# Banded attention by 64-query chunks of eight heads, keys stored in band order, output projections one group late

## The reference

```python
q, gate = jnp.split(rms_norm(x, norm_g) @ w_in, 2, axis=-1)   # 32 query heads of 64
q = partial_rope(q.reshape(B, L, B_Q_HEADS, B_HEAD_DIM), cos, sin)
o = swa_sink_attention(q, k_sh, v_sh, sinks)                  # 4 key heads, 8 query heads each
return x + (o * jax.nn.silu(gate)) @ w_out
# in swa_sink_attention: NC = 8 chunks of 64 queries; a query sees the 16 meta keys,
# its own chunk of keys and the two chunks before it; the softmax has one more term, exp(sink)
e = jnp.exp(sc - m)
return e / (jnp.sum(e, axis=-1, keepdims=True) + jnp.exp(sink - m))
```

## Time and profile before

| | us |
|---|---|
| median of 3 runs | 3215.2 (3215.03 to 3229.05) |
| profiled execution, its own time | 3217.8 |
| span of its records | 3215.9 |
| PE busy (17876 matmul records) | 3057.8 (95%) |
| PEld busy | 2605.3 (81%) |
| DVE busy | 1511.1 (47%) |
| ACT busy | 1021.2 (32%) |
| POOL busy | 1213.6 (38%) |
| mean granted TensorE clock | 0.978 |

### The profile page before, as it was taken

How to read it: one execution, slowest core, us unless ns; L and a number is a source line. 1 busy time by engine, 2 the same in 40 slices (tenths; PEclk the granted TensorE clock), 3 DMA queues, 4 the chain that set the end, 5 groups by cost and what they waited for, 6 DMA issues and landing times.

```text
span 3215.9 us, 44287 instructions
## 1 busy us (share of the span) xinstructions
PE 3057.8 (95%) x17876; PEld 2605.3 (81%) x17876; DVE 1511.1 (47%) x2731; ACT 1021.2 (32%) x1572; POOL 1213.6 (38%) x888
## 2 busy tenths in 40 slices
PE   7999999999999888999999999799999999999986
PEld 7999999999999887877778777777777777787754
DVE  6444343434435376445454556723233234354556
ACT  4322223132222353323233233532323232233342
POOL 4344343434434242231423324644343343344421
PEclk9999999999999999999999999799999999999998
DMA  4121221212222121121211213222222222221211
GB/s 159 67 92 66 79 79 66 93 66 79 79 79 79 66 73 53 53 79 40 92 53 55 77 40 125 92 92 79 79 81 85 84 79 75 83 82 66 80 64 66
DMA packets 36958, 247.63 MB, mean 77 GB/s; under 512 B 3970, under 2 KB 4115, under 8 KB 8212
## 3 DMA queue, kind: packets, MB, share of 16 engines
q1 hardware_dynamic: 35728, 241.37, 22.1%
q10 hardware_dynamic: 1028, 3.44, 0.3%
HBM read 240.60 MB, written 4.19 MB: 76 GB/s over the span
## 4 chain that ended last, share of the span: by engine, by line
PE 79%; DVE 13%; DVEq 3%; issue 2%; ACT 2%; DMA 0%; ACTq 0%; SPq 0%; POOL 0%
PE pj L281 17%; PE pj L285 17%; PE pj L287 17%; PE pj L312 5%; PE pj L316 5%; PE pj L314 5%; DVE xl L359 2%; DVE arena L405 2%; PE pa L503 1%; PE pa L465 1%; DVEq L407 1%; PE pj L842 1%; PE pa L851 1%; PE pa L865 1%; DVE arena L617 1%
## 5 line engine op out<-in xcount | busy, mean ns | idle before, releaser
L1952 POOL TENSOR_TENSOR wl<-raw,wh 128x512 fp32r<-128x512 f32 x884 | 1213.4, 1403 | 1967.0 <-ACT wh L257 1967.0
L281 PE MATMUL pj<-xh,wh 128*128 128x264 f32 (+2 forms) x3792 | 1121.9, 343 | 20.6 <-POOL wl L1952 16.2
L285 PE MATMUL pj<-xl,wh 128*128 128x264 f32 (+2 forms) x3792 | 1083.9, 333 | 13.9 <-DVE xl L359 13.9
L287 PE MATMUL pj<-xh,wl 128*128 128x264 f32 (+2 forms) x3792 | 1078.9, 331 | 0.0
L257 ACT ACTIVATE wh<-raw 128x2048 fp32r<-128x2048 f32 x221 | 423.2, 1915 | 1026.6 <-PE pj L287 602.4
L281 PEld LDWEIGHTS pj<-xh,wh 128*128 128x128 f32 x3792 | 654.2, 192 | 100.0 <-issue 32.7
L285 PEld LDWEIGHTS pj<-xl,wh 128*128 128x128 f32 x3792 | 653.0, 192 | 86.5 <-DVE xl L359 21.2
L287 PEld LDWEIGHTS pj<-xh,wl 128*128 128x128 f32 x3792 | 653.5, 192 | 65.7
L338 DVE TENSOR_TENSOR acc<-pj,acc 128x512 f32<-128x512 f32 (+1 forms) x336 | 233.3, 696 | 209.9 <-PE pj L316 208.5
L312 PE MATMUL pj<-oh,wh 128*128 128x264 f32 (+1 forms) x1024 | 311.4, 345 | 19.6 <-DVE ol L732 11.1
L316 PE MATMUL pj<-oh,wl 128*128 128x264 f32 (+1 forms) x1024 | 307.4, 341 | 0.0
(11 more groups left out here) (271 smaller groups left out, 2776.1 us busy)
## 6 DMA issues: line engine op xcount, KB each, us to landing
raw<-in_stream SPq DMA_DIRECT2D x221, 1024.0 KB, 4.8
acc<-in_x SPq DMA_DIRECT2D x8, 528.0 KB, 9.3
out_y<-acc SPq DMA_DIRECT2D x8, 512.0 KB, 2.9
arena<-in_mem ACTq DMA_DIRECT2D x2, 1024.0 KB, 7.0
cst<-in_cst SPq DMA_DIRECT2D x1, 448.0 KB, 13.7
cos<-in_cos_a SPq DMA_DIRECT2D x1, 264.0 KB, 13.8
sin<-in_sin_a SPq DMA_DIRECT2D x1, 264.0 KB, 14.0
cos<-in_cos_b ACTq DMA_DIRECT2D x1, 264.0 KB, 2.9
```

What stands on the lines that cost most here:

```text
L281: pe.matmul(pj[:, pu, b, 0:m], whk, xh[:, k, a:a + m], start=(k == 0), stop=False)
L285: pe.matmul(pj[:, pu, b, 0:m], whk, xl[:, k, a:a + m], start=False, stop=False)
L287: ins = pe.matmul(pj[:, pu, b, 0:m], wlk, xh[:, k, a:a + m], start=False, stop=(k == KD - 1))
L1952: pool.tensor_tensor(wl[:, j, at], raw[:, j, at], wh[:, j, at].bitcast(F32), ALU.subtract).then_inc(s_part if c < LO_PARTS - 1 else s_lo, 1)
```

## The change

Attention now goes by 64-query chunks, with all 8 query heads of a key head in one slot: 8 chunks per g, 32 in all. The keys are stored in extended form (`B_K`), four blocks of 16 meta keys followed by 128 keys, so that the band of a chunk (16 + 3 x 64 = 208 keys, fewer for the first two chunks) is one contiguous range; the values are stored in two forms, blocks of 128 keys (`B_v1`) and blocks of 64 + 16 (`B_v2`). The sink is an extra column of the scores in PSUM, so that maximum, exponential and sum take it along. The weights are divided before they are transposed, and the output is computed with features on partitions. A slot does the output of chunk i-2, the transposes of i-1 and the scores of i; slots stand at every 6th k (g = 0, 3) or every 8th (g = 1, 2), the first at k = 7 of the first gate tile. All four query tiles of a group come first, then the gate tiles with the slots, then the output projection of the group before it; each output sum runs over four 128-feature parts where it ran over two, so there are 64 sums where there were 128. Of the diff, the allocation of tiles, the reordering of weights on the host, the waits of ACT's tile order and the old functions (printed above) are left out.

```diff
+B_CH = SEQ // CHUNK
+B_BAND = NMETA + 3 * CHUNK
+B_PW = B_BAND + 2
...
-B_OUTS = 8 + 32
+B_TILES, B_OUTS = 48, 96
...
+        def b_band(c):
+            if c < 2:
+                return 0, P - CHUNK * c, B_BAND - P + CHUNK * c
+            return (P + NMETA) * (c // 2) + (NMETA - P - NMETA if c % 2 == 0 else -CHUNK), 0, B_BAND
+
+        def b_block1(c):
+            if c == 0:
+                return None
+            return (0, c // 2 - 1) if c % 2 == 0 else (CHUNK + NMETA, c // 2)
+
+        def b_block2(c):
+            if c < 2:
+                return (P, CHUNK + NMETA, 0) if c == 0 else (CHUNK, NMETA, 0)
+            return (P if c % 2 == 0 else 0), CHUNK + NMETA, c - 1
...
+        def b_extend(dve, out, x):
+            dve.tensor_copy(as3(out, NQ)[:, :, NMETA:], as3(x[:, 0:SEQ], NQ))
+            for j in range(NQ):
+                dve.tensor_copy(as3(out, NQ)[:, j, 0:NMETA], x[:, SEQ:T])
 
         def kv_dve(dve):
...
-                    for b in range(2):
-                        dve.tensor_copy(B_k[64 * b:64 * b + 64, 2 * c + a, :], B_x[64 * a:64 * a + 64, :])
+                    b_extend(dve, B_K[64 - 64 * a:128 - 64 * a, c, 1, :], B_x[64 * a:64 * a + 64, :])
...
+            for c in range(2):
+                evac_scaled(dve, B_x, U_KV + 2 + c, c, T).then_inc(s_evac, 1)
+                dve.drain()
+                b_extend(dve, B_ve[c], B_x)
...
+        B_POS = [[7 + 6 * i for i in range(10)], [7 + 8 * i for i in range(10)], [7 + 8 * i for i in range(10)],
+                 [7 + 6 * i for i in range(10)]]
+
+        def b_slot(g, i):
             def f(pe):
+                c, n = i - 2, B_CH * g + i - 2
+                if 0 <= c < B_CH:
+                    pe.wait_ge(s_btf, n + 1)
+                    if n >= 2:
+                        pe.wait_ge(s_bo, n - 1)
+                    full, (_, rows, slot) = b_block1(c), b_block2(c)
                     for a in range(2):
+                        out = (bank1, bank3)[c % 2][64 * a:64 * a + 64, 0:2 * P]
+                        if full is not None:
+                            pe.matmul(out, B_v1[:, full[1], B_HD * g:B_HD * (g + 1)], B_pt1[:, 2 * P * a:2 * P * (a + 1)],
+                                      start=True, stop=False)
+                        ins = pe.matmul(out, B_v2[0:rows, slot, B_HD * g:B_HD * (g + 1)],
+                                        B_pt2[0:rows, 2 * P * a:2 * P * (a + 1)], start=full is None, stop=True)
                     ins.then_inc(s_bpv, 1)
+                c, n = i - 1, B_CH * g + i - 1
+                if 0 <= c < B_CH:
+                    pe.wait_ge(s_bnorm, n + 1)
...
+                    for v in range(4):
+                        if full is not None:
+                            pe.transpose(bank[2][:, P * v:P * (v + 1)], B_p[:, v, full[0]:full[0] + P], ident)
+                        ins = pe.transpose(bank[3][0:rows, P * v:P * (v + 1)], B_p[:, v, at:at + rows], ident)
                     ins.then_inc(s_bt, 1)
+                c, n = i, B_CH * g + i
+                if c < B_CH:
...
+                        pe.wait_ge(s_bq, 4 * g + 4)
+                    at, lo, w = b_band(c)
+                    for mp in range(2):
+                        for a in range(2):
+                            h = slice(64 * a, 64 * a + 64)
+                            ins = pe.matmul(B_sc[:, 2 * a + mp, lo:lo + w], B_qc[h, c, P * mp:P * (mp + 1)],
+                                            B_K[h, g // 2, (a + g) % 2, at:at + w], start=True, stop=True)
                     ins.then_inc(s_bs, 1)
...
+        def b_slot_act(act, g, i):
+            c, n = i - 1, B_CH * g + i - 1
+            if 0 <= c < B_CH:
+                act.wait_ge(s_bt, n + 1)
...
+                    act.activation(B_pt1, bank[2], ACT.Copy)
...
+                act.activation(B_pt2[0:rows, :], bank[3][0:rows, :], ACT.Copy)
...
+                for v in range(4):
+                    act.activation(B_p[:, v, lo:B_BAND + 1], B_sc[:, v, lo:B_BAND + 1], ACT.Exp, scale=B_scale,
+                                   bias=B_nb[:, v:v + 1], accum_out=B_sm[:, v:v + 1])
...
+        def b_slot_dve(dve, g, i, meanwhile=None):
+            c, n = i - 2, B_CH * g + i - 2
+            if 0 <= c < B_CH:
+                dve.wait_ge(s_bpv, n + 1)
+                dve.tensor_copy(B_qc[:, c, :], (bank1, bank3)[c % 2][:, 0:2 * P]).then_inc(s_bo, 1)
+            c, n = i, B_CH * g + i
+            if c < B_CH:
+                lo = b_band(c)[1]
+                dve.wait_ge(s_bs, n + 1)
+                dve.reduce_max(B_mx, B_sc[:, :, lo:B_BAND + 1], AX_X)
                 dve.drain()
+                dve.tensor_scalar(B_nb, B_mx, -B_scale, None, ALU.mult).then_inc(s_bnb, 1)
+            if meanwhile is not None:
+                meanwhile()
+            if c < B_CH:
+                dve.wait_ge(s_bexp, n + 1)
+                dve.reciprocal(B_rc, B_sm)
                 dve.drain()
+                for v in range(4):
+                    dve.tensor_scalar(B_p[:, v, lo:B_BAND], B_p[:, v, lo:B_BAND], B_rc[:, v:v + 1], None, ALU.mult)
                 dve.drain()
+                dve.sem_inc(s_bnorm, 1)
+
+        def b_out(pe, t, u, o_wait, at, hooks={}):
+            for j in range(4):
+                pe.wait_ge(s_hi, t + j + 1)
+                for f in range(4):
+                    pe.wait_ge(s_evac, u + 4 * j + f + 1)
+                    for c in range(4):
...
+                        pe.matmul(out, whk, at[0][:, c, 0:SEQ], start=(c == 0), stop=False)
+                        pe.matmul(out, whk, at[1][:, c, 0:SEQ], start=False, stop=False)
+                        ins = pe.matmul(out, wlk, at[0][:, c, 0:SEQ], start=False, stop=(c == 3))
...
+        def b_pe(pe, g):
+            t, u = T_B + B_T0[g], U_B + B_U0[g]
+            at = {k: i for i, k in enumerate(B_POS[g])}
+            for m in range(1 if g == 0 else 0, 4):
+                proj(pe, t + m, u + m, m % 2, m % 2, SEQ)
+            for m in range(4):
+                proj(pe, t + 4 + m, u + 4 + m, m % 2, m % 2, SEQ,
+                     hooks={k: [b_slot(g, at[KD * m + k])] for k in range(KD) if KD * m + k in at})
+            if g > 0:
+                b_out(pe, t + 8, u + 8, O_B0 + 4 * (g - 1), (ohb, olb),
+                      hooks={(k + 1 - 4 * KD) // 4 - 1: b_slot(g, at[k]) for k in at if k >= 4 * KD})
+            if g == B_KV - 1:
+                b_out(pe, t + 12, u + 24, O_B0 + 4 * g, ob_in_x)
...
+        def b_dve(dve, g):
...
+            for m in range(1 if g == 0 else 0, 4):
...
+                if m == 3:
+                    b_sinks(dve, g)
+                q_read(dve, m, u + m, m % 2)
+            for k in range(4 * KD):
+                if k > 0 and k % KD == 0 and k - 1 not in at:
+                    gate(k // KD - 1)
+                if k in at:
+                    b_slot_dve(dve, g, at[k], (lambda: gate(k // KD)) if k % KD == KD - 1 else None)
```

More of the change, by code:

```diff
@@ L47 @@
 T_KV, U_KV = T_A + A_TILES * A_HEADS, U_A + A_OUTS * A_HEADS
-B_TILES = 12
-B_OUTS = 8 + 32
 T_B, U_B = T_KV + 4, U_KV + 4
-T_MEM, U_MEM = T_B + B_TILES * B_KV, U_B + B_OUTS * B_KV
+B_T0 = [0, 8, 20, 32]
+B_U0 = [0, 8, 32, 56]
+B_TILES, B_OUTS = 48, 96
+B_START = [sum(([1] * 8 + ([1] * 8 + [4] * 4) * 3 + [4] * 4)[:i]) for i in range(B_TILES)]
+T_MEM, U_MEM = T_B + B_TILES, U_B + B_OUTS
 SB_TILES = 10
@@ L167, in build @@
         s_bq = sem("s_bq")
+        s_bsk = sem("s_bsk")
         s_bs = sem("s_bs")
@@ L796, in kv_dve @@
             split_dve(dve, 2, "b_norm", SEQ)
[L797 to L801 removed]
+            q_read(dve, 0, U_B, 0)
         def kv_pe(pe):
@@ new lines, in b_sinks, with gate @@
+        def b_sinks(dve, g):
+            if g == 0:
+                dve.wait_ge(s_bvn, 2)
+            dve.tensor_scalar(B_sc[:, :, B_BAND:B_BAND + 1], as3(par_col("sinks", 4 * g, 4), 4), 1.0 / B_scale, None,
+                              ALU.mult)
+            dve.drain()
+            dve.sem_inc(s_bsk, 1)
+        def b_dve(dve, g):
+            u = U_B + B_U0[g]
+            at = {k: i for i, k in enumerate(B_POS[g])}
+            def gate(m):
+                if m > 0:
+                    b_silu(dve, g, m - 1)
+                gate_read(dve, B_g[:, m, :], u + 4 + m, m % 2, SEQ)
+            for m in range(1 if g == 0 else 0, 4):
+                if g > 0 and m == 0:
+                    for c in range(4):
+                        b_o_lo(dve, g - 1, c, (ohb, olb))
+                if m == 3:
[6 more added lines that the diff above has]
+                    b_slot_dve(dve, g, at[k], (lambda: gate(k // KD)) if k % KD == KD - 1 else None)
+            if 4 * KD - 1 not in at:
+                gate(3)
+            late = [at[k] for k in at if k >= 4 * KD]
+            if g == 0:
+                for m in range(3):
+                    b_gate(dve, m)
+                b_silu(dve, 0, 3)
+                b_gate(dve, 3)
+                dve.drain()
+                return
+            for f in range(KD):
+                if late and f == 2:
```

(25 more changed lines are left out.)

383 lines of the change are left out of this document (151 added, 232 removed).

## The result

The changed kernel takes 3050.7 us (median of 4 runs, 3048.9 to 3053.2); the kernel before, in 4 runs beside it, 3215.1 (3209.9 to 3229.1). The ratio is 0.947, 95% interval 0.945 to 0.949: faster by 5.3%. I had said 3100 us and 3072 to 3150: the direction was right, the time lies 21 us under the range. The profiled execution took 3053.2 us, its span is 3051.5, its mean granted clock 0.983 (0.978 before).

The account below looks back on a forecast made before the run. The layer was taken as bound by what TensorE issues: its 788 us stretch would become 670 (-118), with +2 ahead of it -116, so 3217.8 goes to 3102, 3099 against the median, said as 3100 us; range 3072 to 3150.

Parts of the forecast that it names:

- my 136: Attention's steps on TensorE after the change: 34 us per head group, 136 us for four groups.
- my 6: Head of each group: TensorE misses about 1.5 us waiting for rotated queries, 6 us in all.
- my 670: New length of the banded layer's stretch: 523 + 136 + 6 + 4 + 1 = 670 us, for 788.
- 4 products of 256 columns, 4 x 0.44 = 1.76: Value products of a full slot, priced at 1.76 us; bounds from below 0.88 to above 2.51.
- value products take other than 1.8 us a slot: Stated sign, in the slots' value products, that the prediction is wrong.
- my third rival: Value products: column halves overlap, -12 us by order, -25 fully, giving 3088 to 3075; chance 0.10.
- The change of shape, 0.25 us: TensorE in the slots: each change of operand shape costs 0.25 us; 32 per head group, 8.0 us.
- 80 rows behind 128 are no change of shape: Value products: forecast assumed this; the rival that it is a change adds 21 us, 3121, chance 0.17.
- walking the slots through: VectorE's multiplications against GpSimd's stretch, 2.0 to 7.3 us into a tile: outside it each time, mostly by 0.5 to 2 us.
- I cost this wait at nothing: TensorE's wait for divided weights: softmax chain 4.65 us, return after 6.3 us at close spacing, 1.6 us spare.
- the sigmoid ... ends before the next exponentials are due: ACT between slots: three sigmoid instructions of 512 columns, at most 0.9 us each, end in time.
- a rival of 150 us and more: The 16 gate tiles: lower clock holds, 150 us and 95 us on top of 3100, giving 3345; chance 0.03.

Follow-up runs that it names:

- the kernel with one column tile: Changed kernel with both halves' value products sent to PSUM partitions 0 to 63, second half's output left out: 3075.0 us, ratio 0.9534.
- the eighty-row kernel: Changed kernel with the second block of chunk 1 made 80 rows high instead of 16: 3048.9 us, ratio 0.9463.
- the kernel with the sigmoid behind: Changed kernel with the third gate tile's sigmoid issued behind the slot one k into the next tile, groups 0 and 3: 3053.6 us, ratio 0.9472.

## Why the prediction was wrong, step by step

The layer, in terms: 2256 projection and output matmuls give 2255 distances of 0.2307 us, 520.2 (523 predicted). The 40 slots sum to 95.1 us with 2.0 of waits in them; their first product comes 0.08 us late at 36 starts (3.0; the other four are those with the queries' wait), and the first projection matmul behind a slot takes 0.105 us more than the others (4.2). So attention is 100.3 us for my 136. Waits are 4.8 + 2.0 (the queries' from matmul to matmul) for my 6, the lower clock 0 for 4, "rest" 0 for 1. 520.2 + 100.3 + 6.8 = 627.3 of 627.7 us: 42 below my 670. Two more us are that my stretch of 788 began 12 matmuls late. Counted the same way, 790.0 - 520.2 = 269.8 us lay outside these matmuls before and 107.5 do now, so the whole gain in the layer, 162.3 us, is in attention, its waits and the lower clock before. How it divides between the eight heads of a slot, the narrower band and the new order of the tiles, no run separates.

**The step that failed** is the value products: "4 products of 256 columns, 4 x 0.44 = 1.76", and, in the rival, "By order only the last product of the first half and the first of the second stand side by side". The price of a product was right (0.43 us alone, in the kernel with one column tile); the order was not what limits. The four take 0.86 us. Over the layer the value products cost some 31 us for 53, about 22 of the 42. I had named "value products take other than 1.8 us a slot" as the sign of being wrong, and it came. The mechanism was my third rival, with a chance of 0.10 and 3075 us at full overlap, inside the range; what brought the time out of it is the next term, the change of shape. The row that I missed stood in my own group: in the earlier trace rows four records of L865 stand together, though L868 of the first half lies between the two halves in the program. The halves by rows already ran beside each other past an instruction of the other half.

**The change of shape, 0.25 us,** came from the one place where 16 rows turn into 128. It was 0.36 us less 0.11 for a product of 64 columns, and the 0.11 was too low. In the kernel before, L841 stands behind L839 in one shape:

```profile
1247.43 0.43 PE L839 MATMUL pj<-arena 128*128 128x64 f32 x2
1247.70 0.39 PE L841 MATMUL pj<-arena 128*128 128x64 f32 x2
```

The passes of L841 start 0.11 us apart, and so does its first behind the last of L839: 0.22 for a product, which leaves 0.14 for a change. In the full slot: into the values 0.09, values to transposes 1284.32 - 1283.29 less 4 x 0.215 = 0.17, transposes to scores 1.02 - 8 x 0.109 = 0.15, scores to projection 0.90 - 0.70 = 0.20. Together 0.61 where I had 1.0; over the layer about 14 us (100.3 less the value products is some 69, where I had 136 - 53 = 83). I had a bound from above (more changes) and none from below for this term, and so the range ended at 3072.

**Right:** transposes (0.109 each for 0.11) and scores (0.70 for 0.71); 80 rows behind 128 are no change of shape, which the eighty-row kernel shows; the chain of the softmax (4.55 for 4.65); the wait for queries (1.2 us per group for 1.5); the 5.0 us for output sums go. The multiplications stay clear of GpSimd, all 128 of them at 0.26 to 0.33 us. I had got that by walking the slots through; the rows give the reason more simply. Where a slot comes just ahead of a tile, ScalarE rounds the next weight tile (L264, 1304.76 to 1306.67) only behind the exponentials, and GpSimd starts behind this (1306.75), when the multiplications are over (1305.47). In all 32 slots GpSimd was done some 0.9 us or more before the first multiplication and starts some 0.8 us or more after the last. The negative did meet GpSimd in half of the slots (16 of 32, 0.39 to 1.10 us where it is 0.17) and stayed inside the spare but for 0.2 us in two slots, which is what the kernel with the sigmoid behind has left.

**"I cost this wait at nothing"** (divided weights) held in 30 of the 32 slots that turn divided weights. The spare was 0.6 to 0.8 us and not 1.6, as its cover, the value products, is shorter than I had it; and "the sigmoid ... ends before the next exponentials are due" failed where a slot stands one k into a gate tile, 2 x 1.06 us.

**The clock.** I gave 4 us for it and a rival of 150 us and more. It is 1.00 in all four windows, the 2.4 GHz level, where it was 0.97 to 0.98 in the first two groups before; the longest wait of the layer is now 1.0 us where it was 5.4. The slots' short products didn't lower it.

**Outside the layer.** Ahead of it 1.2 us more (2 predicted). Behind it 3.4 us less, which I hadn't predicted and which no run shows to be an effect of the change: this part takes 1206.2 us in the changed kernel's profile, 1209.3 in the same kernel's second one and 1202.9 to 1210.5 in the others, 1209.6 before. In all 44.3 + 0.8 + 3.4 = 48.5 of the 48.8 us that lie between 3102 (my figure for the profiled execution) and 3053.2.

The Trainium skill, "TensorEngine Tiling (Array Packing)", Key Properties, says that tiles load and multiply in parallel and that a change of mode drains the engine; the trace agrees with the first, with 0.86 us a slot hidden, and has 0.15 to 0.20 us for a change; whether this is a drain no row shows. Here the passes of the second half's L877 start ahead of those of the first half's L879, against the order of the program. The Trainium skill, "TensorE: Matmul & The Clock Gate", The mechanism, says that matmuls start and end in the order of the program, with no reordering; the measurement differs and decides, and the 19.9 us that the kernel with one column tile loses bear it out. Whoever takes that sentence as a price counts these products one behind the other, as I did.

## What to carry to other kernels

Here two products on different halves of the array ran beside each other even with an instruction of the first half between them, as long as no change of shape lay there. In such a case price the longer half alone, and look in the trace whether the records of two halves stand together. Put the short block (16 rows) of both halves next to each other (4.6 us here), and parts of one shape next to the full-width work on either side of the slot (4.8 us). When a cover gets shorter, what it covered has less spare: sum the other engines' queues in their order (sigmoid, copies, exponentials), not each chain by itself.

## What the runs showed of the hardware that I had not expected

- Column halves of fp32 products (128x64 and 80x64 operands, 256 columns) overlap fully: 0.86 us for eight passes, 1.72 when both use the same columns.
- 16 rows behind 128 cost a change (0.58 us from product to product for 0.43 to 0.48) and end the overlap of halves issued one after the other, together 1.27 us a slot; 80 rows behind 128 cost none, and 128x16 transposes between 128x128 ones cost none (0.109 us from each to the next).
- fp32 products of full width and fp32 transposes next to the projection matmuls cost no change: 0.23 us from projection matmul to product, and the slot that ends with transposes is 0.175 us shorter.
- A 4-column VectorE instruction takes 0.17 us alone and up to 1.10 beside GpSimd, while copies of 256 columns from PSUM take 0.41 to 0.43 us either way (14 beside GpSimd, 18 not).
